# Moving sixteen state-space read-out pairs to other units of an attention loop

## What is computed

```python
_, states = lax.associative_scan(combine, (a, bu), axis=1)
y = jnp.real(jnp.einsum('blgp,gcp->blgc', states, c)) + d_skip.astype(f32) * ug
y = jax.nn.gelu(y.reshape(B, L, SSM_WIDTH))
y = y * jax.nn.sigmoid(y @ w_glu.astype(f32))
```

## Time and profile before

| what | value |
|---|---|
| median of three runs | 2240.53 us (2239.04 to 2247.96) |
| the profiled execution, its own time | 2238.76 us |
| its span, first to last instruction | 2236.8 us |
| mean granted TensorE clock over the span | 0.976 of full speed |
| PE busy | 2109.4 us, 94% of the span |
| DVE, ACT, POOL busy | 51%, 36%, 27% of the span |
| HBM traffic | 405.06 MB moved by the DMA engines, mean 181 GB/s |

### The profile page before, as it was taken

The page is one execution under the profiler, slowest core; times in us unless marked ns, Lnnn a source line. Parts: engine busy times, 40 slices in busy tenths (PEclk is TensorE's granted clock), DMA queues, the critical chain, the costliest instruction groups (busy, mean ns, idle before and its releaser), DMA issues. The chain is left out here.

```text
span 2236.8 us, 40759 instructions
## 1 busy us (share of the span) xinstructions
PE 2109.4 (94%) x13609; PEld 1827.7 (82%) x13609; DVE 1140.1 (51%) x3371; ACT 799.8 (36%) x1568; POOL 612.9 (27%) x1047
## 2 busy tenths in 40 slices
PE   7779999999999899998999899999999999999991
PEld 6667889888988778886877788888888888888881
DVE  4743654565465542333567555555555554555544
ACT  4222553454344421113440233333333333333334
POOL 7146555000022200001002233333333333333330
PEclk9999999999999999999999999999999999999996
DMA  4412122121334221102423999999999999999985
GB/s 152 126 38 80 44 81 71 53 58 54 92 103 137 72 71 42 47 28 97 158 76 143 306 306 312 314 315 313 312 310 308 309 307 308 311 315 316 314 274 171
DMA packets 195937, 405.06 MB, mean 181 GB/s; under 512 B 26350, under 2 KB 124742, under 8 KB 178710
## 3 DMA queue, kind: packets, MB, share of 16 engines
q1 hardware_dynamic: 164016, 317.52, 40.1%
q0 software_dynamic: 31680, 86.52, 18.0%
q10 hardware_dynamic: 166, 0.05, 0.0%
HBM read 335.79 MB, written 70.35 MB: 182 GB/s over the span
## 5 line engine op out<-in xcount | busy, mean ns | idle before, releaser
L2485 PE MATMUL ps_gu<-xe,w_raw 128*128 128x160 f32 x4224 | 592.1, 301 | 0.0
L2485 PEld LDWEIGHTS ps_gu<-xe,w_raw 128*128 128x128 f32 x4224 | 577.9, 191 | 0.2
L2524 ACT ACTIVATE w_hi<-w_raw 128x1024 fp32r<-128x1024 f32 x132 | 132.3, 1049 | 299.3 <-DMA w_raw<-in_exp_w_down 299.3
L2449 POOL DMA_INDIRECT scr_acc<-y_rest,out_idx x66 | 106.3, 1611 | 466.6 <-ACT y_rest L2544 466.6
L2567 DVE TENSOR_TENSOR w_lo<-w_raw,w_hi 128x1024 fp32r<-128x1024 f32 x132 | 155.8, 1222 | 152.1 <-ACT w_hi L2524 152.1
L1101 ACT ACTIVATE w_raw_first<-w_raw_first,o_stage 128x128 f32<-128x128 f32 (+1 forms) x192 | 86.3, 450 | 199.8 <-DVE o_stage L1049 198.8
L2449 POOL DMA_INDIRECT scr_acc<-y_main,out_idx x66 | 105.2, 1594 | 98.4 <-ACT y_main L2547 96.0
L2547 ACT ACTIVATE y_main<-ps_ye,gate 128x512 f32<-128x512 f32 x132 | 90.9, 688 | 113.0 <-PE ps_ye L84 113.0
L1780 DVE TENSOR_TENSOR e_idx_f<-ps_xt,e_neg_slot 128x2 f32<-128x2 f32 x64 | 10.2, 159 | 217.3 <-PE ps_xt L1771 217.2
L1761 DVE TENSOR_SCALAR e_sel<-e_slots,e_place 128x256 bf16<-128x256 bf16 x536 | 110.9, 281 | 0.0
L82 PE MATMUL ps_ye<-w_hi,e_h_hi 128*128 128x512 f32 x264 | 110.5, 419 | 0.0
(11 more groups left out here) (433 smaller groups left out, 4908.8 us busy)
## 6 DMA issues: line engine op xcount, KB each, us to landing
w_raw<-in_exp_w_gate SPq DMA_DIRECT2D x66, 1024.0 KB, 8.0
w_raw<-in_exp_w_up SPq DMA_DIRECT2D x66, 1024.0 KB, 7.4
w_raw<-in_exp_w_down SPq DMA_DIRECT2D x66, 1024.0 KB, 8.3
w_raw_first<-in_w_in SPq DMA_DIRECT2D x24, 512.0 KB, 4.6
v_w_raw<-in_w_in SPq DMA_DIRECT2D x48, 256.0 KB, 2.7
merged<-in_x SPq DMA_DIRECT2D x14, 512.0 KB, 4.9
scr_att<-o_stage SPq DMA_DIRECT2D x16, 264.0 KB, 3.0
att_prev<-scr_att SPq DMA_DIRECT2D x16, 264.0 KB, 3.4
```

The lines of the kernel that those rows point to most:

```text
L2449: pool.indirect_dma_start(out=acc_rows[c], out_offset=bass.IndirectOffsetOnAxis(ap=out_idx[j][:, c:c + 1], axis=0), in_=y[:, :], in_offset ...
L2485: ins = pe.matmul(ps_gu[:, 2 * w + c, 0:CAP], w3(raw[j][w])[:, k, P * c:P * c + P], xT[:, k, :], start=(k == 0), stop=(k == KD - 1))
L2524: act.activation(piece_of(hi[j], piece), piece_of(raw[j][DOWN], piece), ACT.Copy).then_inc(hi_made, 1)
```

## The change

It rewrites the list of units that hold a pair. Before, the four turns held two, four, six and four pairs; after it they hold two, three, three and eight, with the last eight pairs in the consecutive units 48 to 55. Since pairs now follow each other unit by unit, the wait of a pair for its PSUM bank is narrowed to the pair that last used the same bank (that of unit w - 2) instead of all pairs before it.

```diff
-        PAIR_AT = (7, 15, 19, 23, 27, 31, 33, 36, 38, 41, 44, 46, 49, 51, 53, 55)
+        PAIR_AT = (7, 15, 21, 27, 31, 37, 41, 45, 48, 49, 50, 51, 52, 53, 54, 55)
...
             pe.wait_ge(ld_op[p % 2], 32 * (p // 2 + 1))
             pe.wait_ge(o_evac, w - 1)
             if w - GU * (NG - 1) in PAIR_AT:
-                pe.wait_ge(s5_evac, p)
+                pe.wait_ge(s5_evac, PAIR_AT.index(w - GU * (NG - 1)) + 1)
```

## The result

Over 11 runs the changed kernel took 2250.15 us in the median (2241.28 to 2256.31), the one before 2241.96 us over 11 runs (2238.15 to 2247.96). The ratio is 1.0027, with a 95% interval of 1.0016 to 1.0038: 6 us slower, between 4 and 9, and within the 0.5% that I had called no change. The profiled execution of the changed kernel took 2244.51 us, that of the one before 2238.76, so the two traces differ by nearly as much (5.7 us) as the runs do. The forecast was 2244.5, with a range of 2237 to 2251.

A forecast was written before the change was run, and what follows sets the result against it. PE was taken as the bound up to unit 45 of the third group, loads from unit 48 to 56. Terms -3.9 - 1.2 + 10.0 = +4.9 us gave 2243.7 (2245.4 by the run median); forecast 2244.5, range 2237 to 2251.

The forecast's parts named there:

- The likeliest case: Two operand slots and their loads set the pace of units 48 to 56; +4.9 us in sum, chance 0.77.
- the second term: Units 44 to 48: earlier pairs let DVE's last low part end sooner, score of unit 48 1.2 us earlier (0 to 2).
- the third: Units 48 to 56: eight pairs wait for loads into two slots, 24.6 us instead of 14.57, a loss of 10.0.
- Pairs out of the full stretch: Before unit 42: seven pairs instead of ten, 1.30 us each, a gain of 3.9 us (3.5 to 3.9).
- the rival in which this gain fails: Before unit 42: PE waits for DVE and ACT, perhaps 2 of 3.9 us left; +7 or 2247 us, chance 0.06.
- the rival of the low clock: Units 48 to 56: clock falls in the waits between pairs; +12 us or 2252, chance 0.07.
- The rival that loads don't bind: Units 48 to 56: slots turn in under 3.7 us, 17.1 us for the stretch; -2.6 or 2238, chance 0.10.
- The landing: Larger half of a pair's load lands 3.0 to 5.0 us after issue, median 3.6; a slot turns in 5.4 us.

The follow-up runs named there:

- the changed kernel with the addition held back: Changed kernel with GpSimd's last addition of merge 4 waiting for DVE's last key copies; one trace, units 48 to 56 took 27.09 us.
- the one with a single pair in 47: Kernel before with one pair moved from unit 46 to 47, and the narrowed wait; ratio 1.0002 to the kernel before.
- the kernel with six buffers: Changed kernel with own operand buffers for pairs 10, 11, 12 and 15, GLU loads queued last; ratio 0.9989 to the kernel before.
- six buffers, addition held back: As six buffers, pair in 47, but GpSimd's last addition of merge 4 waits for DVE's last key copies; ratio 0.9984 to the kernel before.
- six pairs in the last turn: Changed kernel with six pairs in units 50 to 55 and two more in turn 2, still two slots; one trace, units 48 to 56 took 19.26 us.
- six buffers, pair in 47: The kernel with six buffers, its pair of unit 45 moved to 47, loads of pairs 9 to 13 before merge 4's store; ratio 0.9988 to the kernel before.

## Why the prediction was right

*The case.* The likeliest case came true with its mechanism: eight pairs in a row outrun two slots, and PE waits for operands. 2244.5 was forecast and 2250.15 measured, or 2248 by the ratio and the median of before. By the median it lies near the upper end of the range, 2251. The sum is better compared from trace to trace: +4.9 forecast, +5.7 measured over the whole and +5.28 up to unit 56. That it came so close is in part luck: the second term was 1.0 us too hopeful and the third 0.6 us too dark, and most of this cancels.

*Pairs out of the full stretch.* -3.9 forecast, -3.91 measured at unit 42. DVE and ACT kept up, as turn 0 had said, so the rival in which this gain fails is out.

*The second term was mis-sized:* -1.2 forecast, -0.2 measured at unit 48. Its first half was right in kind. With the pair of unit 44 gone PE waits 0.55 us for the exponential of unit 43, as worked out, and the score of unit 45 is 0.35 us better off, where I had about 0.6.

```profile
693.36 0.33 PE L985 MATMUL ps_mixer<-ident,w_raw_first 128*128 128x128 f32 x1 [0.55 <-ACT w_raw_first L1101]
```

The step that failed is "Following score, pair, transposes and values through I get a start at 700.3 and an end at 703.1". On that scale the start came at 700.65 and the end at 704.03. So 0.35 us of the error is the start, and the rest, 0.6, the length: 3.38 us where I had 2.8. The end is set by GpSimd, whose merge 4 runs beside the casts and holds them. The low parts moved ahead by 0.66 us on the scale of the trace before and merge 4 did not (697.66 us and, on that scale, 697.67), so the casts now met its last addition for longer. I had the row of the casts (1.37 us for two) and took it for their normal length. The row beside it, of the kernel before, is this one; the first of the two casts ended at 703.78, 0.28 us behind it:

```profile
702.23 1.27 POOL L1263 TENSOR_TENSOR att_prev<-att_prev 128x512 f32<-128x512 f32 x1 [0.18 <-POOL att_prev L1261]
```

*Units 48 to 56.* +10.0 forecast, +9.39 measured (23.96 us against 24.6). A slot turns in 5.1 to 5.7 us against 5.4. Counted from the score of unit 48, pair 11 ended at 13.5 us, where 13.6 was forecast, and the two turns of its slot behind it took 10.2 us instead of 10.8. The order of the queue with the GLU loads between 10 and 11 did what was worked out: pair 11 waits longest, 2.54 us, and the load behind GLU landed 5.1 us after its issue. The clock was milder than forecast: it was halved for 3.41 us, not for 6.82 as in the earlier trace rows, and then stayed at full with PE busy 13.79 of 20.10 us. So the rival of the low clock did not come true in this kernel, through waits of 0.35 to 2.54 us. It did in the changed kernel with the addition held back, in a wait of 5.00 us, and in the one with a single pair in 47, in a wait of 3.17.

*The rival that loads don't bind* is the kernel with six buffers. It had been given -2.6 against the kernel before; the experiment shows -2.2 (-4.19 up to unit 48 and +1.97 behind it, where -5.1 and +2.5 were forecast).

*The landing.* Of the larger loads of pairs 10 to 15, five landed in 3.1 to 3.7 us, and that of pair 11, behind GLU, in 5.1. The measured rows of before were the right base. The estimate of 2.6 us for 256 KB comes from the formula in the Trainium skill, DMA: Bandwidth & Descriptors, section "Anatomy of one DMA", which the page gives for loads issued through GpSimd; the loads of this case are issued by SyncE, and in all eleven traces none of 256 KB for a pair landed in less than 2.8 us.

*Left open:* whether the few us by which whole executions differ behind unit 56 depend on the list at all. From unit 56 to the first matmul of the experts the traces have 524.8 to 531.6 us in no order that follows the edits, and no experiment was made on that. The 5.28 us up to unit 56 account for the 6 us of the ratio in the main, and for the 8.2 us between the two medians only in part.

## What to carry to other kernels

Work that is moved out of a stretch where an engine is full into one where it is idle brings its transfers along: count how fast its buffers can turn (release, issue, landing, use) and divide by their number before you set its pace. With two slots that turn in 5.3 us, a pair every 1.87 us was not to be had; with six buffers it was. And read the queue as its own program: a load waits for everything written before it, so one load of a later stage, or one store that waits for a slow engine, can cost more than the work that was moved.

## What was not expected

*A cast on DVE stands behind GpSimd's addition.* In ten of the eleven traces at least one of the two last casts, each 0.42 us by itself, ended 0.28 to 0.29 us after a tensor_tensor on GpSimd: it took 0.92 us in the kernel before, 1.38 in the changed one, 1.42 in both kernels with a pair in 47 and GpSimd free to run, and 0.95 with the addition held back and the one before it in flight. In the eleventh no addition ran beside the casts, and both took 0.42. It goes the other way too: in the changed kernel the first cast began 0.04 us before GpSimd's last addition, and that addition took 1.51 us instead of 1.27 (1.51 or 1.52 in four more traces with that order). The operations with two inputs on DVE just ahead (L954, one input in PSUM) kept their 0.73 and 0.76 us beside the same operations of GpSimd. The Trainium skill, SBUF — State Buffer, section "Who interferes with whom", says that DVE and GpSimd share one pair of ports as an exclusive lock, that a cast on DVE can take it, and that the second to ask stands until the first is done; the traces agree with it, with the 0.28 us on top. It is easy to miss, because the timeline of DVE shows a long instruction and no wait.

*The clock behind the wait before unit 48 does not follow the length of that wait.* It was halved for 6.82 us in the kernel before and for 3.41 in the changed one, with waits of 2.38 and 2.04 us, and not at all behind one of 1.44 (six buffers, addition held back). But it was also halved for 6.83 us behind 2.04 (six pairs in the last turn) and for 3.41 behind 2.42 (six buffers, pair in 47), and stayed full behind 1.94 (one pair in 47). Of the eight traces in which it fell there, the three with 6.82 or 6.83 us have no pair in unit 48 and the five with 3.41 have one; no experiment was made on that. What it costs is seen in the two kernels with six buffers and a pair in 47, in which PE does the same work in that stretch: 16.58 us with the halved spell and 15.08 without, as much as the edits that were meant to move it.
